# Small VectorE copies removed, and the gate stage's rows and banks shared out anew

## The reference

```python
def peer(h, w_pq, sub_keys, expert_u, expert_v):
    q = (h @ w_pq).reshape(B, S, PEER_HEADS, 2, PEER_QHALF)          # 8 heads
    s = jnp.einsum('bshjd,hjnd->bshjn', q, sub_keys)                 # 128 keys for each half j
    v1, i1 = lax.top_k(s[..., 0, :], 16)
    v2, i2 = lax.top_k(s[..., 1, :], 16)
    cand = v1[..., :, None] + v2[..., None, :]                       # 16 x 16 sums
    cidx = i1[..., :, None] * N_KEYS + i2[..., None, :]
    top_s, pos = lax.top_k(cand, 16)
    idx = jnp.take_along_axis(cidx, pos, axis=-1)                    # the chosen experts
    gate = jax.nn.softmax(top_s, axis=-1)
    # out = sum over the 8 * 16 chosen experts e of gate_e * gelu(u_e . h) * v_e
```

## Time and profile before

| | us |
|---|---|
| median of 3 runs | 2257.02 (2256.85 to 2258.37) |
| span of the profiled execution | 2255.3 |
| TensorE busy | 2016.3 (89%) |
| VectorE busy | 1362.9 (60%) |
| ScalarE busy | 663.8 (29%) |
| GpSimd busy | 537.9 (24%) |
| select stage, TensorE's first to last unit | 474.8 to 726.1 |
| gate stage, first to last `first_hits` | 730.3 to 940.6 |

### The profile page before, as it was taken

One profiled execution on the slowest core, in us unless ns is written; L12 is line 12 of the kernel. 1 busy time (PEld: TensorE's weight loads), 2 busy tenths in 40 slices (PEclk: granted clock), 3 DMA queues, 4 the chain that ended last, 5 costly groups with the idle time before them and its releaser, 6 DMA issues.

```text
span 2255.3 us, 26216 instructions
## 1 busy us (share of the span) xinstructions
PE 2016.3 (89%) x9280; PEld 1657.1 (73%) x9280; DVE 1362.9 (60%) x2292; ACT 663.8 (29%) x1010; POOL 537.9 (24%) x289
## 2 busy tenths in 40 slices
PE   5998786879996666699999999999999999999997
PEld 5777555658774555588788888888888888888886
DVE  6545577349996999755454455455455444544544
ACT  4113343243222666511221222222122122212212
POOL 2877423036775777500000000000000000000000
PEclk7899577979998999999999999999999999999999
DMA  7353001222232655555233224224323322422330
GB/s 313 108 207 123 1 1 63 87 107 80 80 119 75 201 164 162 157 213 189 93 148 131 93 110 169 93 93 159 120 93 133 146 93 96 178 98 93 149 130 37
DMA packets 124155, 276.62 MB, mean 123 GB/s; under 512 B 4817, under 2 KB 70353, under 8 KB 116561
## 3 DMA queue, kind: packets, MB, share of 16 engines
q1 hardware_dynamic: 124112, 276.10, 33.9%
HBM read 233.10 MB, written 42.99 MB: 122 GB/s over the span
## 4 chain that ended last, share of the span: by engine, by line
PE 57%; DVE 0%; ACT 0%; DVEq 0%; issue 0%; ACTq 0%
PE bank L1810 26%; PE bank L1836 25%; PE bank L1825 6%; DVE u_raw L1797 0%; DVE rows L1783 0%; ACT L1722 0%; DVE u L1731 0%; DVEq L1583 0%; ACT u L1675 0%; ACT v_raw L1718 0%; DVE rows L1763 0%; DVE rows L1774 0%; ACT act_out L1700 0%; ACTq L1583 0%; DVE rstd L1793 0%
## 5 line engine op out<-in xcount | busy, mean ns | idle before, releaser
L1810 PE MATMUL bank<-actT,u 128*128 128x512 f32 x2592 | 596.6, 391 | 6.8 <-DVE u L1731 4.0
L1810 PEld LDWEIGHTS bank<-actT,u 128*128 128x128 f32 x2592 | 489.7, 189 | 109.4 <-DVE u L1731 4.2
L1836 PE MATMUL bank<-v_parts,w 128*128 128x512 f32 x2496 | 570.0, 389 | 0.0
L1836 PEld LDWEIGHTS bank<-v_parts,w 128*128 128x128 f32 x2496 | 468.6, 188 | 97.1
L1763 DVE TENSOR_TENSOR rows<-rows,bank 128x512 f32<-128x512 f32 x208 | 142.4, 687 | 256.8 <-PE bank L1836 256.8
L1682 ACT ACTIVATE v_parts<-v_raw 128x1024 fp32r<-128x1024 f32 x104 | 109.6, 1054 | 450.8 <-DVE rows L1763 450.4
L1390 PE MATMUL bank<-actT,hl 128*128 128x512 f32 x864 | 212.7, 406 | 31.2 <-POOL hl L1237 28.0
L1742 DVE TENSOR_TENSOR weighed<-act_out,group_gates 128x512 f32<-128x512 f32 x105 | 72.7, 693 | 272.6 <-ACT act_out L1686 272.6
L1390 PEld LDWEIGHTS bank<-actT,hl 128*128 128x128 f32 x864 | 167.2, 196 | 70.8 <-POOL hl L1237 18.4
L1739 DVE TENSOR_TENSOR v_parts<-v_raw,v_parts 128x1024 fp32r<-128x1024 f32 x128 | 156.2, 1220 | 93.2 <-DMA group_gates<-expert_gates 32.2
L1569 PE MATMUL bank<-onehot 128*128 128x128 f32 x1024 | 132.6, 284 | 85.7 <-POOL onehot L1477 85.7
(11 more groups left out here) (241 smaller groups left out, 2077.4 us busy)
## 6 DMA issues: line engine op xcount, KB each, us to landing
u_raw<-in_u SPq DMA_DIRECT2D x27, 2048.0 KB, 7.5
v_raw<-in_v SPq DMA_DIRECT2D x26, 2048.0 KB, 7.5
expert_gates<-gates SPq DMA_DIRECT2D x16, 2048.0 KB, 8.7
group_gates<-expert_gates SPq DMA_DIRECT2D x32, 1024.0 KB, 6.9
wada<-in_w_ada SPq DMA_DIRECT2D x24, 1024.0 KB, 6.7
v_raw<-in_v SPq DMA_DIRECT2D x24, 512.0 KB, 3.4
raw<-in_u SPq DMA_DIRECT2D x20, 512.0 KB, 3.6
raw<-in_w_cols SPq DMA_DIRECT2D x16, 512.0 KB, 7.2
```

The costliest lines, as they stand in the source:

```text
L1810: last = nc.tensor.matmul(m.psum[j % banks][:], u[:, p, j, kc * P:(kc + 1) * P], m.actT[:, q, kc, :], start=(kc == 0 and i == 0), stop=(kc ...
L1836: last = nc.tensor.matmul(m.psum[2 + p % 6][:], w[:, x, j, t * P:(t + 1) * P], v[:, z, j, half * S:(half + 1) * S], start=(j == 0 and i == 0),
```

## The change

In the select stage `best` and `posf` are gone: `top16` writes its values into `top` itself, and the comparison reads the integer `pos`. The two conversions to `vf` move from VectorE to GpSimd, in `codes`, with a wait of GpSimd for its own result (`places_ready`); `vi` is double. `top16` of the scores now only signals `index_ready`, and VectorE waits for `code_ready` before it writes `vi` again. GpSimd's loop over rounds is written out.

In the gate stage `gate_now` is gone: ScalarE reads the gate from `slotsT`. `ACT_ROWS` goes from 2 to 4, so GpSimd scales 4 rows of 8 and ScalarE 4. ScalarE evicts the first bank of a round, VectorE the second (`read_second_half`), two rounds late, between the second one-hot and the next `first_hits`. `gates_read` becomes a pair of semaphores, one for each evicting engine. VectorE's and ScalarE's loops are written out, 64 rounds.

```diff
-ACT_ROWS = 2
+ACT_ROWS = 4
@@ select, GpSimd
-                pool.wait_ge(vf_ready, k)
+                pool.wait_ge(index_ready, k)
+                g.tensor_scalar(vf[:, b, 0], vi[:, b, 0:TT, :], float(NKEY), None, ALU.mult).then_inc(places_ready, 1)
+                g.tensor_copy(vf[:, b, 1], vi[:, b, TT:, :]).then_inc(places_ready, 1)
+                pool.wait_ge(places_ready, k * 2)
                 candidate_sums(g, code[:, b], vf[:, b, 0], vf[:, b, 1]).then_inc(code_ready, 1)
...
+            for k in range(1, ROUNDS - 1):
+                round_(k, (k - 1) % 2, RAW - 1)
@@ select, VectorE
-                top16(pair, 2 * TT, rest, v, vi)
                 if h >= 2:
-                    dve.wait_ge(hit_coded, 2 * h - 2)
-                V.tensor_scalar(vf[:, h % 2, 0], vi[:, 0:TT], float(NKEY), None, ALU.mult)
-                V.tensor_copy(vf[:, h % 2, 1], vi[:, TT:]).then_inc(vf_ready, 1)
+                    dve.wait_ge(code_ready, h - 1)
+                top16(pair, 2 * TT, rest, v, vi[:, h % 2], index_ready)
                 st.then(dve, candidate_sums(V, cand, v[:, 0:TT], v[:, TT:]))
-                top16(cand, TT, cand2, best, pos)
-                V.tensor_copy(top[:, :, h, :], best[:])
-                st.then(dve, V.tensor_copy(posf[:], pos[:]))
+                top16(cand, TT, cand2, top[:, :, h, :], pos)
@@ gates, ScalarE
                 for u in range(pool_n, ROUND):
+                    at = (i * rounds + b) * ROUND + u
                     last = nc.scalar.activation(onehot1[:, b % BUFS, u, :], hits[:, b % BUFS, :, u], ACT.Copy,
-                                                scale=gate[:, b % BUFS, u:u + 1])
+                                                scale=slotsT[:, 2, at:at + 1])
...
-                for c in range(CHUNKS):
-                    act.wait_ge(gated, i * (rounds * CHUNKS) + (b * CHUNKS + c + 1))
...
+                act.wait_ge(gated, i * (rounds * CHUNKS) + (b * CHUNKS + 1))
+                at = b * ROUND % TB
+                nc.scalar.activation(gates[:, k, :, at:at + PER],
+                                     m.psum[CHUNKS * (b % BUFS)][:].rearrange("p (t j) -> p j t", t=PER),
+                                     ACT.Copy).then_inc(gates_read[0], 1)
@@ gates, SyncE
-                    sp.wait_ge(gates_read, p * (2 * TB // PER) + ((k + 1) * (TB // PER)))
+                    for c in range(CHUNKS):
+                        sp.wait_ge(gates_read[c], p * (2 * TB // ROUND) + ((k + 1) * (TB // ROUND)))
@@ gates, VectorE
-                    V.tensor_copy(gate[:, b % BUFS, :], slotsT[:, 2, n])
+            def read_second_half(r):
+                i, b = divmod(r, rounds)
+                k = b * ROUND // TB % 2
+                if i >= 1 and b * ROUND % TB == 0:
+                    dve.wait_ge(stored[k], i * 16)
+                dve.wait_ge(gated, (r + 1) * CHUNKS)
+                at = b * ROUND % TB + PER
+                V.tensor_copy(gates[:, k, :, at:at + PER],
+                              m.psum[CHUNKS * (b % BUFS) + 1][:].rearrange("p (t j) -> p j t", t=PER)
+                              ).then_inc(gates_read[1], 1)
...
+                if r >= 2:
+                    read_second_half(r - 2)
@@ gates, TensorE
-                            pe.wait_ge(gates_read, i * (rounds * CHUNKS) + ((b - BUFS) * CHUNKS + c + 1))
+                            pe.wait_ge(gates_read[c], i * rounds + (b - BUFS + 1))
```

More of the change, by code:

```diff
@@ L1316, in _, with top16 @@
             st = m.dve
[L1318 removed]
+            def top16(values, count, replaced, largest, where, placed=None):
                 for r in range(count):
@@ L1332, in top16 @@
                     last = V.max_index(where[:, r, 8:16], largest[:, r, 8:16], replaced[:, r, :])
-                st.then(dve, last)
+                if placed is not None:
+                    last.then_inc(placed, 1)
+                else:
+                    st.then(dve, last)
             def codes(h):
@@ L1507, in body @@
-            def body(i, first):
+                act.wait_ge(gated, i * (rounds * CHUNKS) + (b * CHUNKS + 1))
[3 more added lines that the diff above has]
+                                     ACT.Copy).then_inc(gates_read[0], 1)
+            for i in range(pairs):
                 for b in range(rounds):
-                    scale_rows(i, b, first)
+                    scale_rows(i, b)
@@ L1510, in body @@
                     if b >= 1:
-                        read_gates(i, b - 1, first)
-                    elif not first:
-                        read_gates(i - 1, rounds - 1, False)
-            body(0, True)
-            with act.Fori(1, pairs) as i:
-                body(i, False)
-            read_gates(pairs - 1, rounds - 1, False)
+                        read_gates(i, b - 1)
+                    elif i >= 1:
+                        read_gates(i - 1, rounds - 1)
+            read_gates(pairs - 1, rounds - 1)
@@ L1536, in _ @@
             m.dve.then(dve, V.tensor_copy(first_bf[:], slotsT[:, 0, :]))
-            def body(i, first):
-                for b in range(rounds):
-                    if not (first and b < BUFS):
-                        dve.wait_ge(gated, i * (rounds * CHUNKS) + (b + 1 - BUFS) * CHUNKS)
-                    n = bass.ds(i * (rounds * ROUND) + b * ROUND, ROUND)
-                    V.tensor_copy(gate[:, b % BUFS, :], slotsT[:, 2, n])
-                    V.tensor_tensor(hits[:, b % BUFS], iota_bf[:],
-                                    first_bf[:, n].unsqueeze(1).to_broadcast([P, NKEY, ROUND]), ALU.is_equal
-                                    ).then_inc(hits_ready, 1)
-                    V.tensor_tensor(onehot2[:, b % BUFS], iota[:].unsqueeze(1).to_broadcast([P, ROUND, NKEY]),
-                                    slotsT[:, 1, n].unsqueeze(2).to_broadcast([P, ROUND, NKEY]), ALU.is_equal
-                                    ).then_inc(second_ready, 1)
@@ new lines, in _ @@
+            for r in range(pairs * rounds):
+                b = r % rounds
+                if r >= BUFS:
+                    dve.wait_ge(gated, (r + 1 - BUFS) * CHUNKS)
+                n = slice(r * ROUND, (r + 1) * ROUND)
+                V.tensor_tensor(hits[:, b % BUFS], iota_bf[:],
+                                first_bf[:, n].unsqueeze(1).to_broadcast([P, NKEY, ROUND]), ALU.is_equal
+                                ).then_inc(hits_ready, 1)
+                V.tensor_tensor(onehot2[:, b % BUFS], iota[:].unsqueeze(1).to_broadcast([P, ROUND, NKEY]),
+                                slotsT[:, 1, n].unsqueeze(2).to_broadcast([P, ROUND, NKEY]), ALU.is_equal
+                                ).then_inc(second_ready, 1)
+                if r >= 2:
+                    read_second_half(r - 2)
@@ L1555, in _ @@
+            for r in range(pairs * rounds - 2, pairs * rounds):
+                read_second_half(r)
         @block.tensor
```

31 lines of the change are left out of this document (9 added, 22 removed).

## The result

| | us |
|---|---|
| changed kernel, median of 4 runs | 2205.32 (2202.89 to 2206.42) |
| kernel before beside it, median of 4 | 2257.69 (2256.85 to 2261.97) |
| ratio | 0.9764, 95% interval 0.9749 to 0.9778 |
| span of the profiled execution | 2203.6 (before 2255.3) |

The kernel is 52 us faster. The forecast was 2217.0, with a range down to 2207: the sign was right, the gain three tenths larger than the 40.0 forecast, and the time 1.7 us outside the range.

A forecast was written before the change was run, and what follows sets the result against it. The gate stage's exclusion chain bounds: first_hits 0.54 + one-hot 1.13 + GpSimd 1.06 = 2.73 us a round instead of 3.34. Over 64 rounds 39.0, plus 1.0 in select: 2257.0 - 40.0 = 2217.0 us, range 2207 to 2231.

The forecast's parts named there:

- What bounds the stage: Gate stage: a round is a chain of first_hits 0.62, second one-hot 1.13 and GpSimd 1.59, summing to 3.34 us.
- no exclusion: Rival, gate stage: GpSimd is just slow, 1.65 us for 512 elements, ScalarE bounds at 2.45; 2199 us, chance 0.03.
- GpSimd's term: Gate stage, second one-hot's end to GpSimd's end: 1.06 us instead of 1.59 with 4 rows for 6.
- first_hits' term: Gate stage, GpSimd's end to first_hits' end: 0.54 us instead of 0.62 once the small copy goes.
- a freer select stage or shorter chain: Rival, select or gate stage: more gain than forecast, 2203 to 2210 us, chance 0.07.
- The eviction on VectorE: Gate stage: evicting one bank takes some 0.6 us, hidden in the wait for GpSimd, outside the exclusion, costing nothing.
- ScalarE: Gate stage: 4 rows and one eviction take 2.34 us, 2.45 a round, under the chain's 2.73.
- The stores: Gate stage: stores land in 9.3 us at most, buffers are wanted again after about 10.9, leaving 1.6 us.
- slower rival: Gate stage: written-out loops' code fetches stall behind stores, up to 9.3 us each; 2263 us at 5 stalls; chance 0.04.
- The select stage: Select: waits move from the removed converts to the candidate sums; 1.75 + 1.3 won, 2 lost, 1 us gained.

The follow-up runs named there:

- 8 rows: Changed kernel with GpSimd scaling all 8 rows of a round and ScalarE none; 2284.01 us in one run.
- 6 rows: Changed kernel with GpSimd scaling 6 rows and ScalarE 2, the small copy still away; 2251.33 us, ratio 0.9973.
- select stage alone: Changed select stage with the gate stage of the kernel before; 2255.61 us, ratio 0.9986.
- 5 rows: Changed kernel with GpSimd scaling 5 rows and ScalarE 3; 2238.52 us, ratio 0.9902.
- 3 rows: Changed kernel with GpSimd scaling 3 rows and ScalarE 5; 2211.16 us in one run.
- no GpSimd: Changed kernel with VectorE making the scaled rows, GpSimd doing nothing in the gate stage, ScalarE evicting both banks; 2245.13 us, ratio 0.9939.
- 4 and 3 in turn: Changed kernel with GpSimd scaling 4 rows in even rounds and 3 in odd, ScalarE 4 and 5; 2204.92 us, ratio 0.976.
- small copy put back: Changed kernel with the small VectorE copy of the gate put back ahead of first_hits, its output unread; 2213.08 us, ratio 0.9802.
- ScalarE's rows alone: Kernel before with only ACT_ROWS raised to 4; small copy stays, ScalarE evicts both banks; 2216.03 us, ratio 0.9818.
- 8 rows of 64 keys: Changed kernel with GpSimd scaling 8 rows but only the first 64 keys, ScalarE none, other products left out; 2224.74 us in one run.

## Why the prediction was wrong, point by point

**What bounds the stage** was right: a chain of three pieces that exclude each other. That the three terms add up to the period shows nothing, as they are distances between the same ends. What shows it is that each piece keeps its size while the starts move: GpSimd ended 1.58 to 1.60 us behind the one-hot in all 64 rounds before, and 0.93 to 0.98 in the changed kernel. The kernel with 8 rows speaks most clearly against *no exclusion*: GpSimd's operation is 2.89 us long, VectorE's own work 1.21 + 0.68 + 0.68 = 2.57, TensorE's 2.05, ScalarE only evicts, and still the round takes 3.69. *No exclusion* had put the changed kernel at 2199 us, and by its time of 2205 alone it would lie nearer than the forecast; it is these distances that rule it out. The rule cited from the Trainium skill, "SBUF — State Buffer", section "Who interferes with whom", holds in all of these kernels in which GpSimd works.

**The step that failed is GpSimd's term**, "512 elements at 2.07 ns are 1.06 us". It measured 0.96. I had a rate from two sizes that seemed to agree, 768 elements at 2.07 ns and 1600 at 2.08, took their agreement as proof that there is no fixed part, and took 1.06 as the lower bound. The second was another operation with another pattern, f32 in both inputs and runs of 50, and its 3333 ns were a whole length and not a distance from a release; the agreement was chance. Rows already at hand did not share the rate: 2.39 us for 1024 elements is 2.33 ns each, 3.61 us for 2048 is 1.76. In this operation the cost goes by key: 1.6 to 1.8 ns a row, and some 1.6 ns more a key once the run is longer than 4 (5, 6 and 8 were measured). From 6 rows to 4 that saves 0.63 us, not 0.53. That the term falls at most in proportion to the elements holds only if the price of an element is the same at both sizes, and it was not.

**first_hits' term** was forecast at 0.54 and is 0.488. The copy's slot on the chain was right: 0.08 us was forecast, and 0.07 to 0.08 measured, at 6 rows and by putting the copy back. The further 0.05 comes with GpSimd's 4 rows and was not foreseen. Together with GpSimd's 0.10 this is 0.15 us a round, 64 x 0.15 = 9.6 us, about the miss in the gate stage (39.0 forecast; measured 47.8 in the distances and 0.3 behind the last round). Taken apart, the 0.76 us a round are 0.63 for GpSimd's two rows, 0.08 for the copy and 0.05 for what first_hits gains beside 4 rows. The time fell where the prediction had put "a freer select stage or shorter chain", at 0.07, and by the shorter chain. The prediction also calls itself wrong if the round is under 2.6 us; it is 2.58.

**The eviction on VectorE** was rightly costed at nothing: 0.68 us, hidden, and outside the exclusion. **ScalarE** was rightly off the path: 799.80 - 797.52 = 2.28 us in the round shown, where the forecast had 2.34, and idle for 0.31 before the next. **The stores** landed in 9.3 us at most and nobody waited. **Code**: the page has 21 transfers of 0.34 MB in all again, and no wait is put down to them, so the slower rival did not happen. No run changed the written-out loops alone.

**The select stage** was forecast at 1.0 us and gave 0.5 between the two profiles (3.0 against the one other trace of the old stage). The mechanism is as described: the waits moved from the conversions to the candidate sums, and a part to the comparison.

**What was not foreseen: the expert stage.** The first product with `u` to the end of the span took 1305.1 us before and 1302.3 after, 2.9 us less in code that did not change. TensorE's clock in the windows at the stage's start (the seventh number, of full speed), before, then after, then with the select stage alone:

```profile
948.00:952.00 4.00, 1.88 (x5) 1.49 (x5) 3.15 (x3) 3.65 (x4) 0.00 (x0) 0.66 1.02 292
952.00:956.00 4.00, 4.00 (x11) 3.13 (x10) 1.48 (x2) 0.34 (x1) 0.00 (x0) 0.50 0.82 231
```

```profile
899.00:903.00 4.00, 1.63 (x4) 1.34 (x5) 2.91 (x3) 3.89 (x4) 0.00 (x0) 0.78 0.93 280
903.00:907.00 4.00, 4.00 (x16) 3.21 (x15) 1.72 (x2) 0.11 (x1) 0.00 (x0) 0.79 0.81 248
```

```profile
954.00:958.00 4.00, 1.77 (x4) 1.48 (x5) 3.05 (x3) 3.76 (x4) 0.00 (x0) 0.71 1.04 289
```

In all three TensorE had stood idle for some 4 us before the stage's first product. Before the change the granted clock was at its lower level (1.2 GHz) from 949.3 to 956.1, and once more for 3.4 us from 1109.7; after it only from 901.2 to 904.6. The fourteen traces fall into three groups by when the clock fell, counted from the stage's first product:

| clock fell | lower level from there | again some 160 us later | first product to end | kernels |
|---|---|---|---|---|
| 0.0 to 0.6 us ahead | 3.4 us | no | 1302.1 to 1302.3 | changed (three traces), select alone, 5 rows, 3 rows, no GpSimd, 4 and 3 in turn |
| 0.8 to 1.5 us ahead | 6.8 us | 3.4 us | 1304.8 to 1305.1 | before, small copy put back, ScalarE's rows alone |
| 0.5 to 1.0 us behind | 3.4 us | 3.4 us | 1303.7 to 1303.9 | 6 rows, 8 rows, 8 rows of 64 keys |

A window of the second group, in the kernel with ScalarE's rows alone, whose first product comes at 907.7:

```profile
908.00:912.00 4.00, 4.00 (x10) 3.13 (x11) 3.08 (x3) 1.26 (x2) 0.00 (x0) 0.50 1.03 290
```

So the stage's time goes with where its start falls against the fall of the clock, and not with whether GpSimd or a copy is at work in the gate stage. The three traces of the changed kernel agree to 0.02 us (1302.25 to 1302.27), so for that kernel it was no chance of the execution. What puts a kernel into its group was not tested. Of the kernel before there is one trace only, so it stays open whether the 2.9 us are part of the change in every run.

The account of the two profiles, from unrounded starts: 0.2 us ahead of the select stage, 0.4 from its first product to the first first_hits, 47.8 between the first_hits, 0.3 from the last of them to the expert stage, 2.9 in the expert stage: 51.6, the difference of the spans. In the range's terms: its lower end lay 10 us under the forecast, and 9.1 of unforeseen gain in the gates and 2.9 in the experts, less 0.6 missed in select, went past it.

## What to carry to other kernels

When two engines exclude each other, write down the chain of the pieces between them and read each as the distance from one's end to the other's end, not as the length on the page. Before a piece is resized, get its price from the same pattern at another size; a rate from another operation is neither a value nor a bound. Here one element more in the innermost run cost 0.42 us in one place and 0.21 in the others. A copy that is busy for a long time may be paying a wait that the next instruction will pay instead: only one that stands ahead of work free of the exclusion, or has a slot of its own on the chain, is worth its removal.

## What the runs showed of the hardware that was not expected

GpSimd's multiplication (bf16 by f32, to f32, with the output strided), counted from the end of the VectorE operation that kept it out, costs 5.3, 7.1, 10.4, 12.0 and 15.3 ns for an innermost run of 3, 4, 5, 6 and 8 elements, and 0.05 us an instruction. The fixed part rests on one kernel. Why a run of 5 costs a step more wasn't settled.

A VectorE comparison of 128 f32 elements with two scalars from memory took 0.26 us back to back, about as much as 230 elements of the comparison of two tensors (1024 in 1.135 us).

In select, a chain of short VectorE operations with two inputs loses its turn again and again while GpSimd has operations queued: head 3's first three sums each wait for the end of another GpSimd operation, and the seven took 7.15 us.
